# Choosing the experts of heads 2 to 5 in steps behind the dot products of heads 1 and 2

## The reference, cut to what matters

```python
s1, i1 = lax.top_k(sc[:, :, 0], PEER_TOPK)      # 16 best of 128, first half of the key
s2, i2 = lax.top_k(sc[:, :, 1], PEER_TOPK)      # 16 best of 128, second half
cand = s1[..., :, None] + s2[..., None, :]      # 256 sums for a token and head
top_s, sel = lax.top_k(cand, PEER_TOPK)         # 16 best of 256
eidx = take_along_axis(cidx, sel)               # expert numbers, cidx = i1 * 128 + i2
a = gelu(einsum('td,tkd->tk', x, expert_u[eidx]))
y = einsum('tk,tkd->td', a * softmax(top_s), expert_v[eidx])
```

## Time and profile before

| | us |
|---|---|
| median of 3 runs (3516.3 to 3517.65) | 3516.88 |
| the profiled execution | 3518.44 |
| its span, first to last instruction | 3516.7 |
| busy: PE, DVE, POOL, ACT | 2765.0, 2369.1, 1981.9, 615.2 |

### The profile page before, as it was taken

How to read it: one execution, slowest core, us unless ns; L and a number is a source line. 1 busy time by engine, 2 the same in 40 slices (tenths; PEclk the granted TensorE clock), 3 DMA queues, 4 the chain that set the end, 5 groups by cost and what they waited for, 6 DMA issues and landing times.

```text
span 3516.7 us, 23931 instructions
## 1 busy us (share of the span) xinstructions
PE 2765.0 (79%) x6672; PEld 1221.2 (35%) x6672; DVE 2369.1 (67%) x5146; ACT 615.2 (17%) x1468; POOL 1981.9 (56%) x2100
## 2 busy tenths in 40 slices
PE   8999888766667877766699998887666678787666
PEld 4655443222223323222246554433222233232222
DVE  1435777777777777886514347777777778778864
ACT  1231221111111211111113312211110111111111
POOL 0001366777676767777500014667776767677774
PEclk9989999988889989888899899998888899898898
DMA  4112799999999999999831137999999999999998
GB/s 146 66 48 100 278 404 407 409 409 409 407 409 394 408 408 398 404 408 402 311 138 48 48 116 283 404 407 409 409 409 407 409 393 402 406 402 408 404 408 311
DMA packets 351321, 1164.86 MB, mean 331 GB/s; under 512 B 36690, under 2 KB 66514, under 8 KB 350932
## 3 DMA queue, kind: packets, MB, share of 16 engines
q0 software_dynamic: 294912, 1073.87, 77.2%
q1 hardware_dynamic: 53812, 89.15, 7.2%
q10 hardware_dynamic: 2464, 0.31, 0.1%
HBM read 1161.10 MB, written 2.10 MB: 331 GB/s over the span
## 4 chain that ended last, share of the span: by engine, by line
PE 37%; DMA 27%; POOL 13%; DVE 13%; issue 6%; ACT 3%; DVEq 0%; ACTq 0%; SPq 0%; POOLq 0%
DMA arena<-in_peer_u,rows 15%; DMA arena<-in_peer_v,rows 11%; PE bank L1514 10%; POOL arena L546 7%; POOL arena L537 7%; DVE arena L1011 6%; PE bank L1333 5%; PE yv L1306 5%; PE bank L1306 4%; PE bank L1488 3%; PE yv L1462 2%; DVE yv L1040 2%; ACT arena L740 2%; PE yv L1375 1%; PE bank L1312 1%
## 5 line engine op out<-in xcount | busy, mean ns | idle before, releaser
L1514 PE MATMUL bank<-arena 128*128 128x512 f32 x3072 | 1674.4, 694 | 687.5 <-DMA arena<-in_peer_v,rows 518.8
L1011 DVE CUSTOM_DVE_ANT_0 arena<-arena,xps 128x1024 f32<-128x1024 f32 x1024 | 1240.7, 1215 | 426.7 <-DMA arena<-in_peer_u,rows 398.3
L537 POOL DMA_INDIRECT arena<-in_peer_u,rows x1024 | 973.8, 951 | 566.3 <-issue 254.6
L1514 PEld LDWEIGHTS bank<-arena 128*128 128x128 f32 x3072 | 634.9, 219 | 1718.7 <-DMA arena<-in_peer_v,rows 919.6
L546 POOL DMA_INDIRECT arena<-in_peer_v,rows x1024 | 970.6, 948 | 395.9 <-issue 260.4
L1040 DVE SCALAR_TENSOR_TENSOR yv<-arena,yv 128x1024 f32<-128x1024 f32 x248 | 317.9, 1282 | 46.6 <-DMA arena<-in_peer_v,rows 38.1
L579 ACT ACTIVATE arena<-arena 128x16 f32<-128x16 f32 x64 | 13.9, 218 | 1883.8 <-DVE arena L1011 1883.6
L740 ACT ACTIVATE arena<-keep,arena 128x128 f32<-128x128 f32 x768 | 231.3, 387 | 103.4 <-DVE arena L1027 102.8
L1333 PE MATMUL bank<-xT,arena 128*128 128x128 f32 (+2 forms) x768 | 228.5, 457 | 4.4 <-ACTq L712 3.1
L1306 PE MATMUL yv<-arena,xT 128*128 128x512 f32 (+1 forms) x384 | 167.1, 590 | 0.0
L1306 PE MATMUL bank<-arena,xT 128*128 128x512 f32 (+1 forms) x384 | 161.7, 578 | 4.2 <-DMA arena<-in_w_in 4.2
(11 more groups left out here) (287 smaller groups left out, 1955.8 us busy)
## 6 DMA issues: line engine op xcount, KB each, us to landing
arena<-in_w_in SPq DMA_DIRECT2D x12, 2048.0 KB, 8.8
arena<-in_peer_wq SPq DMA_DIRECT2D x24, 1024.0 KB, 9.6
arena<-in_peer_u,rows POOLq DMA_INDIRECT x1024, 11.1
arena<-in_peer_v,rows POOLq DMA_INDIRECT x1024, 11.2
arena<-in_w_out SPq DMA_DIRECT2D x4, 2048.0 KB, 7.8
arena<-in_ple_wg SPq DMA_DIRECT2D x4, 2048.0 KB, 20.9
arena<-in_mixer SPq DMA_DIRECT2D x2, 2112.0 KB, 19.7
ln<-in_ln SPq DMA_DIRECT2D x8, 512.0 KB, 8.0
```

The lines of the kernel that those rows point to most:

```text
L537: e.indirect_dma_start(urow[i % UR], None, a["peer_u"], bass.IndirectOffsetOnAxis(ap=rows[:, n % RR, k:k + 1], axis=0)).then_inc(u_in[i % ...
L1011: e.tensor_tensor_reduce(r, r, xps[:, :], 1.0, 0.0, ALU.mult, ALU.add, dots[:, n % 2, k:k + 1]).then_inc(u_free, 1)
L1514: ins = e.matmul(bank[m][:, :], diag[:, k, :], vrow[i % VR][:, m * 512:(m + 1) * 512], start=(h == 0 and k == 0), stop=(h == PH - 1 and k ...
```

## The change

Nothing is chosen behind head 0 any more. Behind each of the 16 dot products of head 1 come two steps for heads 2 and 3, first the 13 steps on halves of keys, and from the eighth dot product on those on pairs; behind the dot products of head 2 the same is done for heads 4 and 5. Between two steps on pairs there is a `drain`. From head 3 on everything is as it was, and so are POOL, ACT, PE and SP. `weights(0)` now directly follows `dot_products(0)`. `halves_step` with 10, 13 and `pairs_step` from 15 on do nothing.

```diff
--- before.py
+++ after.py
@@ -1009,7 +1009,16 @@
                         e.wait_ge(u_in[i % UR], (l * (PAIRS * TOPK // UR) + i // UR + 1) * 16)
                         r = urow[i % UR]
                         e.tensor_tensor_reduce(r, r, xps[:, :], 1.0, 0.0, ALU.mult, ALU.add, dots[:, n % 2, k:k + 1]).then_inc(u_free, 1)
-                        if n % 2 == 1 and n + 4 < PAIRS:
+                        if n == 1 or n == 2:
+                            heads = [2 * n, 2 * n + 1]
+                            if k < 7:
+                                halves_step(heads, 2 * k, i + 1)
+                                halves_step(heads, 2 * k + 1, i + 1)
+                            else:
+                                pairs_step(heads, 2 * (k - 7), i + 1)
+                                e.drain()
+                                pairs_step(heads, 2 * (k - 7) + 1, i + 1)
+                        elif n % 2 == 1 and n + 4 < PAIRS:
                             halves_step([n + 3, n + 4], k, i + 1)
                         elif n % 2 == 0 and 0 < n and n + 3 < PAIRS:
                             pairs_step([n + 2, n + 3], k, i + 1)
@@ -1264,14 +1273,7 @@
 
                 for n in range(PAIRS):
                     dot_products(n)
-                    if n == 0:
-                        halves_first([2, 3])
-                        weights(n)
-                        halves_second([2, 3])
-                        pairs_first([2, 3])
-                        pairs_second([2, 3])
-                    else:
-                        weights(n)
+                    weights(n)
                     if n % PH == 0 and n > 0:
                         add_y(n // PH - 1)
                     if n in PLE_AT:
```

## The result

| | us |
|---|---|
| before, median of 14 runs (3514.2 to 3521.8) | 3518.89 |
| changed, median of 14 runs (3524.8 to 3528.7) | 3526.33 |
| difference | +7.4 |
| ratio, 95% interval | 1.0024, 1.0016 to 1.0031 |
| changed, profiled execution and its span | 3526.55, 3524.8 |

The change made the kernel slower by 0.24%, 5.6 to 10.9 us. I had forecast +4.6, in a range that reaches from -4 to +11 on the scale of the median I had then (3516.88). It lies just beyond the 7 us up to which I called a change none, where I had given a chance of 0.20, and beyond the likeliest case, which ended at 3523.7.

A forecast was written before the change was run, and what follows sets the result against it. The prediction took the DMA engines' gathers to bound the kernel. It counted 2.3 us lost in each of 2 layers, +4.6, and nothing for the other terms: 3521.5 us on the median's scale, range 3513 to 3528.

The forecast's parts named there:

- likeliest case: Both layers: late row numbers cost 1.0 to 3.4 us a layer, 3518.9 to 3523.7 us; chance 0.55.
- What bounds the kernel: PEER block: DMA engines bound it, moving 1,024 gathers of 512 KB at 409 GB/s, 1.28 us each.
- The 13 us do not reach the DMA engines: Head 1 starts 13.0 us earlier on DVE, but PE holds POOL before v row 8 until 428.28.
- The new wait: Before u row 0 of head 2, POOL waits for L1000's row numbers until 451.2 to 452.2, 4 to 5 us.
- What the DMA engines lose: Row 0 of head 2 lands 1.8 to 3.1 us later, taken as 2.3 a layer.
- the gather moved ahead: U row 8 of head 1 issued at about 413.2; counted as nothing, upper bound 1.3 us a layer.
- the fit that I had set beside it: Gather landing by 2.0 us plus bytes at 436 GB/s; loss some 1.2 us a layer, 2.4 in all; not followed.
- Not made good later: POOL's 4.70 us stall before 472.64 gives back queue, not bytes; the 2.3 us carry to the layer's end.
- Load of head 2 at nothing: DVE's added steps for heads 4 and 5 behind head 2 count 0, upper bound 1 us a layer.
- One sign that I had named as wrong: DMA shares under 1 inside heads 2 or 3 would show the forecast wrong.
- A: Row numbers of head 2 stand before about 449.3, new wait hidden: 0 to -1.3 us a layer; chance 0.20.
- B: From dot product 11 on, steps add waits and drains, numbers come later still: +8.8 us, 3525.7; chance 0.20.
- C: Behind head 0, the 13 us reach the DMA engines: up to -22 us, 3495; chance 0.05.

The follow-up runs named there:

- e3: Kernel before with the whole choice for heads 2 and 3 moved ahead of the weights of head 0; 3519.5 us, 1.0008 of before.
- e2: Changed kernel with three steps instead of two behind each dot product of head 1, a drain behind each; 3517.7 us, 1.0003 of before.
- e6: Changed kernel with the last step (L1000) of heads 2 and 3 moved behind the added row after dot product 15; 3532.3 us, 1.0046 of before.
- e1: Kernel before with only heads 4 and 5 given both kinds of steps behind head 2; 3519.2 us, 1.0005 of before.
- e9: Kernel before, choice ahead of head 0's weights, PE's queries behind v rows, ACT's gelu and identities before late copies; 3501.6 us, 0.9960 of before.

## Why the prediction was right in its account and short in its size

- *What bounds the kernel*: held. Inside the block the DMA engines move 409 GB/s after as before; what was lost is time in which they moved less.
- *The 13 us do not reach the DMA engines*: held. One gather went ahead (409.49), then PE held POOL. e3 tells it alone. PE and ACT, which hold it, keep their order:

```profile
405.57 13.97 PE L1335 MATMUL bank<-xT,arena 128*128 128x512 f32 x32 [0.61 <-ACT arena L619]
...
422.29 17.29 PE L1516 MATMUL bank<-arena 128*128 128x512 f32 x36 [2.75 <-ACT arena L740]
...
419.58 0.59 ACT L599 COPY arena<-bank 128x512 f32<-128x512 f32 x1 [6.22 <-PE bank L1335]
...
420.28 3.62 ACT L740 ACTIVATE arena<-keep,arena 128x128 f32<-128x128 f32 x12
```

- *The new wait*: held, 4.85 us less the 0.3 of an ordinary step, where 4 to 5 were forecast. L1000 itself was forecast for 451.9 and stood at 453.2 on the scale of before. That is the 1.5 us by which PE's first v rows came slower (below), less the little by which my list was too long. e2 and e6 show it as the cause, by undoing and by lengthening it.
- *What the DMA engines lose*: the mis-sized term, 2.3 us a layer forecast. Its first half is right: row 0 of head 2 took 4.0 us to land in the emptied queue (forecast 4.2 to 4.5) and landed at 457.6 on the scale of before, 4.0 later than there, 1.5 of them from PE's slower start. That leaves 2.5, within the 1.8 to 3.1 forecast. But I stopped at the first row, and priced what follows it at nothing. The second u row:

```profile
arena<-in_peer_u,rows POOLq DMA_INDIRECT x1, 4.0
...
arena<-in_peer_u,rows POOLq DMA_INDIRECT x1, 6.2
```

Issued at 452.37 it took 6.2 us and landed at 458.57, 4.7 us behind the first, where two gathers need 2.56 at full rate. The windows agree: from 452 to 460 the mean is 304 instead of 409 GB/s, which is 2.1 us of transfers. Together that is 4.6 a layer, and the whole hole read at once gives the same, 248 GB/s from 448 to 460, 4.7 us; in layer 1 it is some 4.2 (341 GB/s from 2202 to 2230 against 402 before). Less up to 1.3 for the gather moved ahead that is about 3 to 4.7, where 2.3 was forecast; the medians gave 3.7. So the difference of two landing times, 6.7 less 4.3, is not the whole price of an emptied queue: the refill cost about as much once more. The kernel before had shown it, behind its own stall of 27.48 us: 323 GB/s over 12 us, 2.5 us of transfers short. I had not priced it:

```profile
448.00:460.00 12.00, 12.00 (x40) 6.36 (x41) 7.86 (x19) 4.07 (x11) 7.68 (x9) 1.00 0.73 248
...
428.00:440.00 12.00, 12.00 (x30) 5.30 (x29) 11.79 (x34) 1.65 (x5) 8.98 (x10) 1.00 0.92 323
```

(The first row is of the changed kernel, the second of the kernel before.) In both stretches POOL issues a gather every 1.24 us from its restart on, and the other queues move 0.02 MB in the first and 0.10 in the second, so other traffic is not the cause; what keeps the rate down while the queue fills, no run here shows. By the fit that I had set beside it, from the Trainium skill ("DMA: Bandwidth & Descriptors", Anatomy of one DMA — SWDGE (gpsimd) path), 3.2 us for such a gather, the sum would have been lower still. The landing of 4.0 us measured here is above it.
- *Not made good later*: held. The stall ahead of v row 8 of head 1 shrank from 4.70 to 0.51 us, and the stretches stayed 5.7 and 7.3 us longer.
- *Load of head 2 at nothing*: e1 agrees within its interval, and its DMA share stayed at 1.02 to 1.03. One sign that I had named as wrong did come, DMA shares under 1 inside head 2 (0.84 to 0.96 up to 460), but from the refill, and the 409 GB/s came back only there.
- *Rivals*: A (hidden) is out by e2 and e6. B's place and price were nearly met in the total, but not its mechanism: the steps took no longer than forecast. That the time lies in the stated range is owed to the room left for B, since my own case ended at +6.8. C's way was open only in e9, together with a change of order on PE and ACT, and gave 14 to 16 of its 22 us.
- The stretches of the profiled execution add up to 13.0 us more than before, the medians to 7.4. Some 3.3 of the 13 are PE's slower start in both layers (below), an estimate from POOL's waits of 15.62 and 15.89 us against 14.09 to 14.10 in e2 and e3. e1 has that slow start in both layers too and no late numbers: against its stretches the changed kernel is 3.5 and 4.8 us longer, 8.3 in all. That part is hardly the clock's: from PE's first matmul to POOL's gather it took 3.76 and 4.03 us in the changed kernel, 3.75 and 3.61 in e1. How much of the 7.4 us of the medians is PE's slower start stays open, since each kernel has one profiled execution. The rest of the program was 4.9 us shorter in this execution; e2 has the short mixer as well and e6, with the steps of the changed kernel, has not, so it does not come from the change.

## What to carry to other kernels

Starting an engine earlier helps only as far as the next in-order queue lets it: follow the freed slot through every wait ahead of the scarce transfer, and find all holds, since taking one away may give nothing or less. An index that a gather needs is due when its issuing queue gets there, one ring ahead of its use; work hidden behind the last loads before it can be the latest of all. When a saturated queue runs dry, price the refill as well as the gap.

## What the runs showed of the hardware that I had not expected

PE's granted clock in the first v rows of head 0 differs between executions and layers of the same program. In the changed kernel it was 0.50, the lower of its two levels (1.2 GHz), in the first 3 us of these rows in layer 0 and in the first 6 in layer 1; at the same point of the work the kernel before and `e3_piece_first` had 1.00, the upper level (2.4 GHz):

```profile
422.30:425.30 3.00, 3.00 (x4) 1.44 (x5) 2.92 (x7) 2.88 (x7) 0.00 (x0) 0.50 0.81 277
...
2180.50:2186.50 6.00, 5.99 (x7) 2.50 (x8) 5.82 (x13) 2.90 (x7) 1.66 (x2) 0.50 0.47 150
```

```profile
426.05:429.05 3.00, 3.00 (x7) 1.40 (x8) 2.96 (x9) 2.97 (x8) 1.71 (x2) 1.00 1.07 355
```

```profile
425.70:428.70 3.00, 3.00 (x7) 1.36 (x8) 2.96 (x7) 2.97 (x8) 0.81 (x1) 1.00 0.79 269
```

(Changed kernel, kernel before, `e3_piece_first`.) PE had been idle for 2.7 us ahead of these rows in all of them, and its clock had been 1.00 during the query before. With the full clock POOL got its slot 2.2 us after PE's first matmul (426.05 to 428.28), in the changed kernel 3.8 us after it (422.29 to 426.05). `e1_load_head2` had the half clock in both layers and `e2_three_steps` in neither. `e6_numbers_later` had it in layer 0 and not in layer 1, in one execution, with POOL's wait there 15.61 and 14.09 us. So it is not the new steps alone that bring it; what decides between the two is open.
